# Router logits per group of four tiles, with the split router weights as the stationary operand, inside the output projection of a hybrid layer

## The reference, cut to what matters

```python
mixed = jnp.concatenate([_rms(out_sb, sb_norm_g), _rms(out_lru, lru_norm_g)], axis=-1)
h = h + mixed @ w_out                                   # output projection, 1024 x 1024
u = _rms(h, norm2_g)
g_logits = u @ w_group + b_group                        # 4 groups
f_logits = u @ w_fine + b_fine                          # 32 experts, 8 in each group
```

## Time and profile before

| | |
|---|---|
| median of three runs | 4404.73 us (4402.45 to 4404.73) |
| the profiled execution | 4407.07 us, its span 4405.3 us |
| TensorE's granted clock, mean | 0.981 |
| busy: TensorE, VectorE, ScalarE, GpSimd | 4172.4, 2817.8, 2489.9, 598.0 us |
| output matmuls of `mix`, first to last start | 2378.8 to 2838.0 us of the span |
| first instruction of `route` on TensorE | 2856.74 us |

### The profile page before, as it was taken

How to read it: one execution, slowest core, us unless ns; L and a number is a source line. 1 busy time by engine, 2 the same in 40 slices (tenths; PEclk the granted TensorE clock), 3 DMA queues, 4 the chain that set the end, 5 groups by cost and what they waited for, 6 DMA issues and landing times. The chain is left out here.

```text
span 4405.3 us, 83265 instructions
## 1 busy us (share of the span) xinstructions
PE 4172.4 (95%) x28239; PEld 3126.2 (71%) x28241; DVE 2817.8 (64%) x3211; ACT 2489.9 (57%) x3370; POOL 598.0 (14%) x792
## 2 busy tenths in 40 slices
PE   7999989997998998999998999869999999999997
PEld 6888867774555555555555888758888788888886
DVE  3222235568998998999995555466665655545665
ACT  3222225456887887888885333246655655545665
POOL 0000002221000000000000111103332322223322
PEclk9999999998999999999999999889999999999999
DMA  5535452313001001001103434347666654555673
GB/s 192 180 138 184 149 171 104 125 67 113 31 31 59 30 30 59 31 30 52 35 6 102 150 138 151 113 164 255 216 232 217 230 196 165 199 184 194 239 257 140
DMA packets 308624, 590.25 MB, mean 134 GB/s; under 512 B 38704, under 2 KB 104240, under 8 KB 308400
## 3 DMA queue, kind: packets, MB, share of 16 engines
q1 hardware_dynamic: 257568, 460.82, 29.8%
q0 software_dynamic: 46224, 118.03, 7.7%
q10 hardware_dynamic: 4608, 8.39, 0.5%
HBM read 427.75 MB, written 209.72 MB: 145 GB/s over the span
## 5 line engine op out<-in xcount | busy, mean ns | idle before, releaser
L1173 DVE TENSOR_TENSOR_SCAN att_R<-att_stay,att_R,att_turn 128x1025 f32<-128x1025 f32 x448 | 1025.3, 2340 | 40.9 <-ACT att_stay L1110 38.9
L1120 ACT ACTIVATE att_RT<-att_rt 128x1024 f32<-128x1024 f32 (+1 forms) x576 | 550.0, 955 | 235.9 <-PE att_rt L1058 195.8
L1058 PEld LDWEIGHTS att_rt<-ident,att_R 64*128 64x128 f32 x8448 | 318.7, 139 | 354.1 <-issue 350.4
L1110 ACT ACTIVATE att_stay<-att_z 128x1024 f32<-128x1024 f32 (+2 forms) x576 | 546.9, 950 | 19.7 <-PE att_z L1046 15.8
L1073 PE MATMUL att_out<-att_RT,att_dv 128*64 128x512 f32 (+3 forms) x2304 | 523.1, 575 | 0.2
L1058 PE MATMUL att_rt<-ident,att_R 64*128 64x64 f32 x8448 | 386.9, 228 | 75.3 <-ACT att_RT L1120 61.0
L1601 DVE TENSOR_TENSOR ew_lo<-ew_raw,ew_hi 128x1024 fp32r<-128x1024 f32 x384 | 444.0, 1218 | 21.9 <-ACT ew_hi L1594 13.5
L1594 ACT ACTIVATE ew_hi<-ew_raw 128x1024 fp32r<-128x1024 f32 x384 | 373.7, 1047 | 103.4 <-PE ex_down L1989 97.1
L241 PE MATMUL qkv_out<-u_u_hi,qkv_w_hi 128*128 128x512 f32 x768 | 308.7, 402 | 11.9 <-DVE u_u_lo L232 11.9
L241 PE MATMUL qkv_out<-u_u_hi,qkv_w_lo 128*128 128x512 f32 x768 | 300.2, 391 | 0.0
L241 PE MATMUL qkv_out<-u_u_lo,qkv_w_hi 128*128 128x512 f32 x768 | 299.7, 390 | 0.0
(11 more groups left out here) (287 smaller groups left out, 8447.6 us busy)
## 6 DMA issues: line engine op xcount, KB each, us to landing
ew_raw<-in_w_e_gate SPq DMA_DIRECT2D x32, 2048.0 KB, 9.1
ew_raw<-in_w_e_up SPq DMA_DIRECT2D x32, 2048.0 KB, 9.9
ew_raw<-in_w_e_down SPq DMA_DIRECT2D x32, 2048.0 KB
u_x<-in_x SPq DMA_DIRECT2D x32, 512.0 KB, 5.9
s_u_hi<-u_u_hi SPq DMA_DIRECT2D x8, 2048.0 KB, 11.8
s_u_lo<-u_u_lo SPq DMA_DIRECT2D x8, 2048.0 KB, 16.4
mix_x<-in_x SPq DMA_DIRECT2D x32, 512.0 KB, 5.0
s_h<-mix_h SPq DMA_DIRECT2D x32, 512.0 KB, 3.7
```

Of the source, the lines that this page charges most:

```text
L1058: last = nc.tensor.transpose(rt[:, half, qt, h, :], R[lanes, n % 3, qt, h, s * P:(s + 1) * P], k.ident[lanes, lanes])
L1110: done = nc.scalar.activation(stay[:, step % 4, :, 0:width], z_pair[:, :, 0:width], ACT.Sigmoid, scale=-scale)
L1120: nc.scalar.activation(RT[:, s, first:, :, :, :].rearrange("p t h half q -> p (t h) half q"), turned_pair, ACT.Copy).then_inc(rt_copied, 1)
L1173: nc.vector.tensor_tensor_scan(joined(R[:, n % 3, s, :, :]), joined(stay[:, step % 4, :, :]), joined(turn[:, s, :, :]), R[:, (n - 1) % 3, ...
```

## The change

The router is done once for a group of 512 tokens, in the first two tiles of the next group.

- The router's weights are split once (`split_router`): `wr` has 128 columns for each of the eight chunks, the hi part in columns 0 to 35, the lo part in 64 to 99, zeros elsewhere. They are the stationary operand.
- For each chunk c of the 1024 features, four transposes bring that chunk of the four tiles into one bank of 512 tokens (`pe_turn`). ScalarE copies it to `u2_hi`, VectorE subtracts for `u2_lo`; both have two buffers. Two matmuls of 512 columns, `wr` with hi and `wr` with lo, add into one bank (`pe_logits`), 16 of them in a group.
- The bank holds the sums for both parts of the weights, transposed. ScalarE copies it, TensorE turns it back with four transposes (`pe_back`), and VectorE adds bias, columns 0 to 35 and columns 64 to 99 in two operations (`dve_logits`).
- TensorE's parts are placed by `pe_router` after the blocks of 12 matmuls of tiles 0 and 1 (places 0 to 7): chunks are turned after places 1 to 4, multiplied after places 2 to 5, and turned back after place 7. Tiles 2 and 3 have none.
- Since `u2` of the old group is still read in tile 0, the square, root and `u2` of tile 0 (`act_square`, `dve_u2`) move to tile 1, behind the last chunks. `select` moves from the end of tile 0 to the end of tile 1.
- Group 0 has no router work in it. After the last group all eight places run one behind another, with nothing beside them.

```diff
+            def pe_turn(pe, G, chunks):
+                for c in chunks:
+                    if c == 0:
+                        pe.wait_ge(u2_ready, G * RING + 1)
+                        pe.wait_ge(logits_ready, G)
+                    pe.wait_ge(u2_lo_ready, G * DC + c + 1)
+                    for t in range(RING):
+                        last = nc.tensor.transpose(tr[c % 2][:, t * P:(t + 1) * P], u2[:, t, c * P:(c + 1) * P], k.ident[:])
+                    last.then_inc(u2_transposed, 1)
+            def pe_logits(pe, G, chunks):
+                for c in chunks:
+                    if c == 0:
+                        pe.wait_ge(logits_t_ready, G)
+                    pe.wait_ge(u2_lo_ready, G * DC + c + 3)
+                    for n, part in enumerate((u2_hi, u2_lo)):
+                        last = nc.tensor.matmul(logits[:], wr[:, c, :], part[:, c % 2, :], start=(c == 0 and n == 0),
+                                                stop=(c == DC - 1 and n == 1))
+                    last.then_inc(logits_done, 1)
+            def pe_back(pe, G):
+                pe.wait_ge(logits_t_ready, G + 1)
+                pe.wait_ge(u2_lo_ready, G * DC + DC + 2)
+                for t in range(RING):
+                    last = nc.tensor.transpose(tr[0][:, t * P:(t + 1) * P], logits_t[:, t * P:(t + 1) * P], k.ident[:])
+                last.then_inc(turned_back, 1)
+            def pe_router(pe, G, t, half, n):
+                place = 4 * t + 2 * half + n
+                if place in range(2, 6):
+                    pe_logits(pe, G, range(2 * place - 4, 2 * place - 2))
+                if place in range(1, 5):
+                    pe_turn(pe, G, range(2 * place - 2, 2 * place))
+                if place == 7:
+                    pe_back(pe, G)
...
-                        if half == 0:
-                            pe_transposes(pe, T - 1, (t - 1) % RING)
-                    if first and t == 1:
-                        pe.wait_ge(params, 48)
-                    pe_logits(pe, T - 1, (t - 1) % RING)
+                            if not first:
+                                pe_router(pe, G, t, half, n)
...
+            def act_router(act, G, chunks):
+                for c in chunks:
+                    act.wait_ge(u2_transposed, G * DC + c + 1)
+                    act.wait_ge(logits_done, G * DC + c + 1)
+                    nc.scalar.activation(u2_hi[:, c % 2, :], tr[c % 2][:], ACT.Copy).then_inc(u2_hi_ready, 1)
+            def act_logits_t(act, G):
+                act.wait_ge(logits_done, G * DC + DC + 2)
+                act.wait_ge(turned_back, G)
+                nc.scalar.activation(logits_t[:], logits[:], ACT.Copy).then_inc(logits_t_ready, 1)
...
-                    if not (first and t == 0):
-                        act_u2_t(act, T - 1, (t - 1) % RING)
+                    if t == 0 and not first:
+                        act_router(act, G, range(6))
+                        continue
+                    if t == 1 and not first:
+                        act_router(act, G, (6, 7))
+                        act_square(act, G, 0)
+                        act_logits_t(act, G)
+                    act_square(act, G, t)
...
+            def dve_router(dve, G, chunks):
+                for c in chunks:
+                    dve.wait_ge(u2_hi_ready, G * DC + c + 1)
+                    nc.vector.tensor_tensor(u2_lo[:, c % 2, :], tr[c % 2][:], f32(u2_hi[:, c % 2, :]),
+                                            ALU.subtract).then_inc(u2_lo_ready, 1)
+            def dve_logits(dve, G):
+                dve.wait_ge(turned_back, G + 1)
+                sums_of = tr[0][:].rearrange("p (t n) -> p t n", n=P)
+                result = k.logits[:].rearrange("p (t n) -> p t n", n=NR)
+                nc.vector.tensor_tensor(result, sums_of[:, :, 0:NR], k.b_router[:].unsqueeze(1).to_broadcast([P, TT, NR]),
+                                        ALU.add).then_inc(biased, 1)
+                dve.wait_ge(biased, G)
+                nc.vector.tensor_tensor(result, sums_of[:, :, 64:64 + NR], result, ALU.add).then_inc(logits_ready, 1)
...
...
+                    if t == 1 and not first:
+                        dve_router(dve, G, (6, 7))
+                        dve_u2(dve, G, 0)
                     dve.wait_ge(x_loaded[t], G * 16 + 16)
...
                     for n in range(2):
+                        if t == 0 and not first:
+                            dve_router(dve, G, range(2 * n, 2 * n + 2))
                         cols = slice(n * GT, (n + 1) * GT)
...
-                    if not (first and t == 0):
-                        dve_logits(dve, T - 1, (t - 1) % RING)
...
+                    if t == 0 and first:
+                        split_router(dve)
                     if t == 0 and not first:
+                        dve_router(dve, G, (4, 5))
+                        continue
+                    dve_u2(dve, G, t)
+                    if t == 1 and not first:
+                        dve_logits(dve, G)
                         select(dve, G - 1)
```

More of the change, by code:

```diff
@@ L1236, in mix @@
             u2 = nc.alloc_sbuf_tensor_at("mix_u2", [P, RING, D], F32, offset=MIX_TOP - 8 * D * 4)
-            u2_t = sb("mix_u2_t", [P, 2, DC, P])
+            u2_hi, u2_lo = sb("mix_u2_hi", [P, 2, GT], F32R), sb("mix_u2_lo", [P, 2, GT], F32R)
+            wr = nc.alloc_sbuf_tensor_at("mix_wr", [P, DC, P], F32R, offset=MIX_TOP - 4 * D * 4)
+            logits_t = nc.alloc_sbuf_tensor_at("mix_logits_t", [P, GT], F32, offset=MIX_TOP - 3 * D * 4)
             iota_i = sb("mix_iota_i", [P, P], I32)
@@ L1249, in mix @@
             tr = [ps(f"mix_tr{i}", [P, GT]) for i in range(2)]
-            logits = ps("mix_logits", [P, NR])
+            logits = ps("mix_logits", [P, GT])
             params = sem("mix_params")
@@ L1270, in mix @@
             u2_transposed = sem("mix_u2_transposed")
-            u2_t_ready = sem("mix_u2_t_ready")
+            u2_hi_ready, u2_lo_ready = sem("mix_u2_hi_ready"), sem("mix_u2_lo_ready")
+            wr_ready, wr_step, biased = sem("mix_wr_ready"), sem("mix_wr_step"), sem("mix_biased")
             logits_done = sem("mix_logits_done")
+            logits_t_ready = sem("mix_logits_t_ready")
+            turned_back = sem("mix_turned_back")
             logits_ready = sem("mix_logits_ready")
@@ L1337, in select @@
                 g_dist = k.g_dist[:, bass.ds(G * TT * NGRP, TT * NGRP)].rearrange("p (t n) -> p t n", n=NGRP)
-                dve.wait_ge(logits_ready, G * TT + TT + 1)
+                dve.wait_ge(logits_ready, G + 2)
                 link(V.tensor_reduce(s_max[:], logit[:, :, 0:NGRP], AX.X, ALU.max))
@@ L1437, in pe_group @@
                             end.then_inc((first_done, second_done)[half], 1)
-                        if half == 0:
-                            pe_transposes(pe, T - 1, (t - 1) % RING)
-                    if first and t == 1:
-                        pe.wait_ge(params, 48)
-                    pe_logits(pe, T - 1, (t - 1) % RING)
+                            if not first:
+                                pe_router(pe, G, t, half, n)
             @block.tensor
             def _(pe):
-                groups(pe, pe_group)
-                pe_transposes(pe, NT - 1, RING - 1)
-                pe_logits(pe, NT - 1, RING - 1)
+                pe_group(pe, 0, True, False)
+                pe.wait_ge(wr_ready, 1)
+                with pe.Fori(1, NG - 1) as G:
+                    pe_group(pe, G, False, False)
+                pe_group(pe, NG - 1, False, True)
+                for place in range(8):
+                    pe_router(pe, NG, place // 4, place // 2 % 2, place % 2)
             def act_inputs(act, G, t):
@@ L1463, in act_squares, with act_square @@
                 nc.scalar.activation(sq[:, t % 2, :, :], raw[t], ACT.Square).then_inc(sq_ready, 1)
[L1465 to L1470, removed]
+            def act_router(act, G, chunks):
[7 more added lines that the diff above has]
+                nc.scalar.activation(logits_t[:], logits[:], ACT.Copy).then_inc(logits_t_ready, 1)
+            def act_square(act, G, t):
+                T = G * RING + t
+                act.wait_ge(h_ready, T * 2 + 4)
+                act.wait_ge(rms2_ready, T + 1)
+                act.wait_ge(squared, T + 1)
+                act.wait_ge(u2_transposed, G * DC + DC)
+                nc.scalar.activation(u2[:, t, :], h[:, t, :], ACT.Square, accum_out=sum2[:]).then_inc(squared, 1)
+                act.wait_ge(squared, T + 2)
+                act.wait_ge(rinv2_ready, T + 1)
+                nc.scalar.activation(rms2[:], sum2[:], ACT.Sqrt, scale=1.0 / D, bias=k.eps[:]).then_inc(rms2_ready, 1)
             def act_group(act, G, first, last):
@@ L1499, in _ @@
                 groups(act, act_group)
-                act_u2_t(act, NT - 1, RING - 1)
+                act_router(act, NG, range(DC))
+                act_logits_t(act, NG)
             def dve_low(dve, G, t):
@@ L1505, in dve_low, with dve_u2 @@
```

(36 more changed lines are left out.)

7 lines of the change are left out of this document (removed).

## The result

The changed kernel takes 4422.56 us in the median (4418.79 to 4424.1, six runs) against 4403.27 before (4399.75 to 4404.73, six runs): ratio 1.0043, 95% interval 1.003 to 1.0056. It is slower, by 19.3 us where 11.9 were forecast. The profiled execution has a span of 4421.4 us, 16.1 more than before.

What follows compares the result with a forecast made beforehand. TensorE's instruction stream was taken as the bound. Loop: -25.6 saving + 18.9 stall + 6.0 clock = -0.7; with tail +12.6, +11.9 us, so 4417 us from 4404.73. Range 4402 to 4429, the forecast's own 4411 to 4424.

Steps and rivals of the forecast that it cites:

- rival 2: Whole stage: clock falls in all seven groups, none of 0.66 absorbed, whole tail at half clock; +24.3, 4429 us; chance 0.15.
- TensorE's own stream: In the loop: 78.3 us of logits and transposes removed, 52.7 added, so TensorE's stream gets 25.6 us shorter.
- rival 4: Long matmuls below the output's pace, or first hand-over a microsecond or more late per group; +7 us and beyond; chance 0.04.
- The stall: Before tile 3's output matmuls: TensorE waits for mix_lo behind select, 2.7 us in each of seven groups, 18.9 us.
- the two additions: VectorE, ahead of select: two 144-column additions lengthen the chain by 0.66 us, part perhaps absorbed; stall between 2.4 and 3.1.
- The clock: Behind the seven stalls: a fall costs 1.7 us; bounds none and 11.9, half taken, 6.0 us.
- The tail: After the last group: four tiles' router work uncovered, growth 8.7 at full or 16.5 at half clock; 12.6 us taken.
- four matmuls: In the tail's circle for a pair of chunks: 0.93 us within 3.4 at full clock, 1.86 within 5.2 at half.
- Same: Whole stage: stall comes, clock never falls for it, tail recovers at once; 0 to +2, 4405 to 4407 us; chance 0.26.
- Clearly slower: The name of rival 2: all seven clock falls and the whole tail at half clock; 4429 us; chance 0.15.
- Faster: In the loop: mix_lo of tile 3 comes in time and TensorE's saving stays; -13, 4392 us; chance 0.08.
- hand-overs in tiles 0 and 1: Chunk copies by ScalarE and subtractions by VectorE finish before TensorE needs them; costed at nothing, tightest cover 0.3 us.

Runs made afterwards that it cites:

- e1: Changed kernel with select moved from the end of tile 1 to the middle of tile 2, behind mix_lo of tile 3: 4387.36 us, ratio 0.9964.
- e4: Changed kernel with four more 128-column operations in select's chain, 1.3 us, results overwritten: 4435.74 us, ratio 1.0067.
- e2: Changed kernel with twelve extra 512-column matmuls, results unused, on TensorE after the sums of tile 3: 4412.25 us, ratio 1.0019.
- e3: Changed kernel with the tail in single chunks: TensorE turns chunk c + 2 right after the matmuls of chunk c: 4419.55 us, ratio 1.0033.
- e5: Changed kernel with the edits of e1 and e3 together: 4387.65 us, ratio 0.9957.
- e6: The kernel of e5 with sixteen extra 512-column matmuls, results unused, ahead of the tail's first transposes: 4384.97 us, ratio 0.9954.

## Why the prediction was right, point by point

In short: the wait, its releaser and the tail were seen beforehand, but the clock's term was half of what it should have been. The measured 4422.56 us lies 5.6 above the forecast's 4417 and 6.4 below the 4429 of rival 2; stall and clock came out nearer to the rival's terms, saving and tail nearer to the forecast's. Part of it is luck: a tail taken 1.9 us too long hid some of the loop's error.

*The bound and TensorE's own stream: right.* TensorE was busy without a gap before, and the change took 26.7 us out of its stream (25.6 forecast), as the loop of e1 shows. Tiles 2 and 3 take 11.6 us from sums to sums where there is no wait (11.68 summed), tiles 0 and 1 16.1 and 14.8. They do not wait, so rival 4 (the change does not do what it says) is out too.

*The stall: right in place, releaser and size.* Seven waits for `mix_lo` of tile 3, 19.5 us, where 18.9 were summed. Counted from start to start, the measure of the saving, they are 20.4: six times 3.41 us from the sums to the output matmul and once 2.56, where 0.37 is usual. Six idle times are 2.9; the last, 2.05, stands in group 7, which is written out and not part of the loop. e1 shows the cause by taking select out of the way, e4 by lengthening it: 1.3 us in, 1.3 us out.

*What of the two additions would be absorbed: about 0.3 of 0.66.* M + 14.93 became M + 15.3. The forecast lay between the two readings, and so does the result. GpSimd's two additions in another group of the changed kernel, and VectorE's operations beside them:

```profile
2643.99 1.29 POOL L1374 TENSOR_TENSOR mix_sq<-mix_sq 128x512 f32<-128x512 f32 x1 [13.99 <-ACT mix_sq L1491]
2645.36 0.76 POOL L1377 TENSOR_TENSOR mix_sq<-mix_sq 128x256 f32<-128x256 f32 x1
```

```profile
2644.31 1.00 DVE L1345 TENSOR_TENSOR g_dist<-logits,mix_s_max 128x16 f32 x1 [0.16 <-DVE mix_s_max L1344]
2645.34 0.17 DVE L1346 TENSOR_SCALAR mix_s_pen<-g_dist 128x16 f32 x1
2645.55 0.59 DVE L1347 SCALAR_TENSOR_TENSOR mix_s_cand<-mix_s_pen,iota 128x16 f32<-128x16 f32 x1
```

The long ones are now other operations than before, L1345 and L1347 in place of the third and the sixth of the chain, and L1345 again ends as GpSimd's first addition ends, at 2645.3. In e1, where select starts later than both, they take 0.18 and 0.17, and the chain from L1344 to L1365 takes 6.3 us instead of 7.6. The Trainium skill (SBUF — State Buffer, "Who interferes with whom") has such pairs exclude each other for a whole instruction when the VectorE operation has two inputs in SBUF; both long operations have two. These rows agree. The forecast's step from there, "select would still leave GpSimd's second addition at the same time, and the stall would be 2.4", was right in its first half only. Before, select goes on behind that addition with its seventh operation, at M + 6.88:

```profile
2631.20 0.17 DVE L1345 TENSOR_SCALAR mix_s_pen<-mix_s_pen 128x16 f32<-128x16 f32 x1
```

After, it goes on at M + 6.86, but with its fifth (L1348, at 2587.47 above), because the addition now holds the fourth operation and not the sixth. Two operations of 0.2 us more are still to come, and that is the 0.4 us by which `mix_lo` is later.

*The clock: right in kind, the term that was too small.* "I take half, 6.0" was 11.2 us by the seven stretches and 11.9 by the distances beside e2. The step that failed is the choice between the rows of 2.14 and 2.89 us: with 2.05 to 2.91 us of idle time and the sums ahead of it, the clock fell every time. The row nearest to a stall of 2.7 us was the 2.89 one, and it should have carried the term. e2 shows the size by itself: 11 us less with the gaps filled. The loop is then -26.7 + 20.4 + 11.9 = +5.6 of the +5.9 measured, where the forecast had -25.6 + 18.9 + 6.0 = -0.7.

*The tail: right in kind, 1.9 us too much.* 10.7 instead of 12.6. Pairs took 3.9 to 4.3 us, at a granted clock of 0.69, and the levels worked out (3.4 and 5.2) were both too high: the pair from 2852.27 ran at 0.50 throughout and took 4.34 us, and one of e1 (2821.11 to 2824.28) at 1.00 took 3.17. The term at fault is "four matmuls" (0.93, or 1.86 at the half clock). Only two of a pair's four stand behind its second subtraction, which ends at 2855.54; the first two start at 2854.74 and run beside that subtraction. Less two matmuls, the half-clock sum is 4.3. So 16.5 could not come; the slowest tail, that of e2 at 0.61, grew by 11.8. Of the 10.7, the order of TensorE's queue is 1.3 to 1.5 (e3, e5) and the clock 1.9 or more (e6); the 6.6 us by which the tail of e6 (21.07) exceeds the old one (14.48) were not taken apart.

*The rivals.* "Same" needed a clock that never falls and a tail of +8.7. e2 shows the first half, a loop 3.7 us shorter than before (442.31 against 445.98); with its tail of +11.8 it is still 8.4 us over the kernel before, near the bound of 8.8. "Clearly slower" had the clock right and the tail wrong. "Faster" did not come: VectorE's chain had no slack, as its rows said. The hand-overs in tiles 0 and 1, cover 0.3 us, cost nothing: TensorE has no idle time there in any of the traces. The cover itself was not tried.

## What to carry to other kernels

When TensorE's stream is made shorter unevenly, look for the longest thing on another engine that used to lie under the part that shrank, and lay its end against the new, shorter distance: here a chain of 7.6 us was moved into a tile of 11.6, ahead of an operation that TensorE needs at that tile's end. Moving the chain behind the urgent operation turned 19 us of loss into 16 us of gain. A wait on TensorE costs its length and can cost the clock behind it, here 20.4 and 11.9 us: price both, and take the clock's price from the row whose idle time is nearest. In a circle of several engines, sum only what stands behind the last hand-over. Batching also gathers work at the end of a loop, where nothing covers it: 10.7 us here.

## What the runs showed of the hardware that was not expected

- Idle times of 2.05 us with 0.37 us of one-column sums ahead of them were enough for the clock to fall (stretch 2831.34 to 2835.00 at 0.53), while one of 2.14 us in the first stage was not the earlier trace rows. So the length of the idle time alone does not tell the two apart; no run shows what does.
- The same idle time did not cost the same each time: 2.90 us and 2.91 us were followed by losses of 1.5 us in five groups and of 2.7 us in one, and the one ahead of tile 1's sums cost 1.5 us more in e1 to e4 than in the changed kernel. A difference of 1 to 2 us between two single traces can be this alone.
- Sixteen 512-column matmuls ahead of the tail kept the clock at 1.00 through 12.2 us in which TensorE was busy for 8.75; without them (e5) it was 0.80 over 14.05 us.
